# Convolution stage: the remainders of the weight tiles made by GpSimd in place of VectorE

## What is computed

```python
# second block, after the branch y_b (retention) is known up to its projection
u   = a * sigmoid(b)                       # a, b: two projections of the normalised x
c   = causal depthwise convolution of u, 31 taps per feature, + bias
c   = silu(layer_norm(c)) * silu(gate)     # gate: a third projection
y_a = c @ w_conv_proj
y_b = o @ w_ret_proj                       # o: 2048 features wide
m   = sigmoid(g_a) * y_a + sigmoid(g_b) * y_b
x   = x + m @ w_out
x   = rms_norm(x, final_gain)
```

## Time and profile before

| | us |
|---|---|
| median of 3 runs | 4187.54 |
| lowest, highest | 4186.81, 4188.52 |
| profiled execution | 4185.86 |
| its span, first to last instruction | 4184.1 |
| busy: PE | 4028.2 (96%) |
| busy: PEld | 3263.4 (78%) |
| busy: DVE | 2214.5 (53%) |
| busy: ACT | 1341.4 (32%) |
| busy: POOL | 1015.9 (24%) |
| mean granted clock of TensorE | 0.977 |

### The profile page before, as it was taken

One profiled execution on the slowest core, in us unless ns is written; L12 is line 12 of the kernel. 1 busy time (PEld: TensorE's weight loads), 2 busy tenths in 40 slices (PEclk: granted clock), 3 DMA queues, 4 the chain that ended last, 5 costly groups with the idle time before them and its releaser, 6 DMA issues. The chain is left out here.

```text
span 4184.1 us, 63976 instructions
## 1 busy us (share of the span) xinstructions
PE 4028.2 (96%) x26360; PEld 3263.4 (78%) x26360; DVE 2214.5 (53%) x2290; ACT 1341.4 (32%) x1621; POOL 1015.9 (24%) x533
## 2 busy tenths in 40 slices
PE   8999998999999999999999999999999999998799
PEld 6888777778888888877777878888888777776677
DVE  6644644552323232379986554343434477776873
ACT  4333443221212121233212123232323355546612
POOL 3222222333232323200002333132323122221221
PEclk9999999999999999999999999999999999998899
DMA  3111224121112121122333121111111222226641
GB/s 137 61 58 60 104 89 157 61 91 51 71 46 71 46 71 50 56 71 76 121 141 121 66 87 62 47 62 47 62 52 57 93 80 81 80 77 222 222 185 61
DMA packets 114613, 361.15 MB, mean 86 GB/s; under 512 B 12916, under 2 KB 14596, under 8 KB 114248
## 3 DMA queue, kind: packets, MB, share of 16 engines
q1 hardware_dynamic: 81216, 291.89, 20.2%
q10 hardware_dynamic: 33160, 65.72, 4.2%
HBM read 262.97 MB, written 94.58 MB: 85 GB/s over the span
## 5 line engine op out<-in xcount | busy, mean ns | idle before, releaser
L414 POOL CAST b_w_hi<-b_w 128x1024 fp32r<-128x1024 f32 x233 | 274.2, 1177 | 2768.4 <-PE ps L510 2123.5
L510 PE MATMUL ps<-b_hi,b_w_hi 128*128 128x512 f32 x1872 | 750.6, 401 | 25.8 <-DVE b_w_lo L430 11.4
L510 PE MATMUL ps<-b_lo,b_w_hi 128*128 128x512 f32 x1872 | 732.3, 391 | 0.0
L510 PE MATMUL ps<-b_hi,b_w_lo 128*128 128x512 f32 x1872 | 731.6, 391 | 0.0
L416 POOL TENSOR_TENSOR b_w_lo<-b_w,b_w_hi 128x1024 fp32r<-128x1024 f32 x233 | 600.6, 2578 | 18.7
L510 PE MATMUL ps<-h_hT_hi,b_w_hi 128*128 128x512 f32 x1216 | 490.8, 404 | 6.5 <-DVE h_hT_lo L240 4.6
L510 PE MATMUL ps<-h_hT_lo,b_w_hi 128*128 128x512 f32 x1216 | 475.5, 391 | 0.0
L510 PE MATMUL ps<-h_hT_hi,b_w_lo 128*128 128x512 f32 x1216 | 475.2, 391 | 0.0
L510 PEld LDWEIGHTS ps<-b_hi,b_w_hi 128*128 128x128 f32 x1872 | 353.2, 189 | 114.6 <-issue 35.0
L510 PEld LDWEIGHTS ps<-b_lo,b_w_hi 128*128 128x128 f32 x1872 | 353.6, 189 | 79.4 <-issue 8.4
L510 PEld LDWEIGHTS ps<-b_hi,b_w_lo 128*128 128x128 f32 x1872 | 353.4, 189 | 74.8
(11 more groups left out here) (703 smaller groups left out, 6332.6 us busy)
## 6 DMA issues: line engine op xcount, KB each, us to landing
b_w<-in_w SPq DMA_DIRECT2D x277, 512.0 KB, 3.5
scratch_x_park<-xT SPq DMA_DIRECT2D x24, 512.0 KB, 4.6
conv_room<-scratch_gate_park SPq DMA_DIRECT2D x24, 512.0 KB, 4.4
xT<-scratch_x_park SPq DMA_DIRECT2D x16, 512.0 KB, 11.7
scratch_gate_park<-ret_fill_out ACTq DMA_DIRECT2D x32, 256.0 KB, 2.0
scratch_o_park<-ret_o ACTq DMA_DIRECT2D x16, 512.0 KB, 4.0
scratch_gate_park<-rw_fill_out ACTq DMA_DIRECT2D x32, 256.0 KB, 2.1
scratch_sb_park<-rw_fill_out ACTq DMA_DIRECT2D x32, 256.0 KB, 2.0
```

The lines of the kernel that those rows point to most:

```text
L414: pool.tensor_copy(hi, w).then_inc(self.rounded, 1)
L510: ins = pe.matmul(out[:, t], w, y, start=start, stop=stop)
```

## The change

GpSimd's block no longer begins with a wait. It calls `subtract_tile` for the tiles first_tile+2 to o_tile_2+2, 33 of them, each as soon as ScalarE has rounded it, and goes on with `cut_tile` from o_tile_2+3. VectorE's block loses its three calls of `subtract_tile`, of which the first is in the loop and runs 31 times. The rounding stays with ScalarE. (L430 has 44 instructions in the whole execution; the other 11 are in other stages and aren't touched.)

```diff
--- before.py
+++ after.py
@@ -2221,7 +2221,8 @@
 
         @block.gpsimd
         def _(pool):
-            pool.wait_ge(stream.cut, o_tile_2 + 3)
+            for k in range(first_tile + 2, o_tile_2 + 3):
+                stream.subtract_tile(pool, k)
             for k in range(o_tile_2 + 3, out + KD):
                 stream.cut_tile(pool, k)
 
@@ -2399,7 +2400,6 @@
                 if e == 0:
                     for k in range(KD):
                         cut_o(k)
-                stream.subtract_tile(dve, first_tile + 1 + n)
                 if n % nt == 2 and n < tiles:
                     multiply(n // nt)
                 if e >= 1:
@@ -2411,9 +2411,7 @@
             for k in range(KD):
                 cut_o_2(k)
             add(KD - 1)
-            stream.subtract_tile(dve, o_tile_2 + 1)
             take_taps(taps, KD * taps_per)
-            stream.subtract_tile(dve, o_tile_2 + 2)
             for e in range(2):
                 add(KD + e)
             dve.wait_ge(mean_done, 1)
```

## The result

The changed kernel takes 4245.19 us in the median of four runs (4237.72 to 4253.02), against 4187.18 for the kernel before (4186.26 to 4188.52): ratio 1.0139 [1.012, 1.0157], 58 us slower. The forecast was 28 us slower, with a range that ended at 4229: the sign was right, half of the size was missing. The profiled execution, the lowest of the four, took 4237.72 us (span 4235.6), 51.9 above that of before.

What follows compares the result with a forecast made beforehand. VectorE was taken to bound the convolution stage, TensorE following. 64.2 - 33.9 - 1.0 + 2.9 - 4.2 = +28.0 us on 4185.86 gives 4213.9, with the median's 1.7 4215.6, said as 4215; range 4203 to 4229.

Steps and rivals of the forecast that it cites:

- VectorE's queue bounds the stage: Convolution stage, 1809 to 2174 us: VectorE's instructions and waits set its end, TensorE follows; any microsecond gained or lost moves the rest.
- Removed, 33.9 us: VectorE's chain from first tap to convolution end: 30 of the 33 remainders leave it, 1.13 us each.
- A stop costs some 2.14 us: VectorE's taps, two SBUF inputs: each GpSimd subtraction beside them was to cost VectorE's queue 2.14 us; ends 1.91 and 2.41.
- 64.2 - 1.0 + 2.9: Stall terms in the chain: 30 x 2.14, less one beside a PSUM addition, plus o_tile_2+3's cast and subtraction.
- a GpSimd subtraction takes 3.25 us even when it is held up: GpSimd's remainders: TensorE needs a tile only some 11.0 us after its slot is free, so was not to wait.
- VectorE busy without a gap: Sign in the profile: VectorE busy from 1809 us to the last L2105, whose end moves from 2174 to about 2202.
- TensorE's waits: Sign before the mean's matmuls: 11.4 us for L430 gone, all waits from 22.3 to about 50 us, behind ScalarE and before the mean.
- The wait at the cut of the branch output, -4.2 us: VectorE's wait at the first cut, for TensorE and ScalarE, was to vanish as these would be ahead: -4.2 us.
- rival 1: Convolution stage: taps aren't stopped, VectorE sheds 33.9 us, TensorE becomes the bound and regains 18.8 us: 4169; 3 in 100.
- Rival 3: Convolution stage: slower still, each remainder costs the whole 2.41 us, +8, or TensorE's slow spells show, +6: 4221 to 4229; 15 in 100.
- Rival 4: GpSimd's queue: it waits in order for each rounding, its later casts come late, at no extra cost; under 1 in 100.
- The end of the sum: Whole program: +28.0 us on the profiled 4185.86 gives 4213.9; the median of the runs is 1.7 higher, 4215.6.

## Why the prediction was half right

- **VectorE's queue bounds the stage**: right. 56 gaps of 0.11 us in the kernel before made the chain 6.3 us longer.
- **Removed, 33.9 us**: right. With the subtraction replaced by a write the chain lost 26.9, and 33.9 less the 6.6 us of a longer wait is 27.3.
- **A stop costs some 2.14 us**: right, with taps stopped in full at 3.36 to 3.47 us in the changed kernel. In the two kernels with few gaps, 32 instructions were stopped for 64.1 and 63.5 us, for the 66.1 that the sum had (64.2 - 1.0 + 2.9). The Trainium skill (SBUF — State Buffer, Who interferes with whom) says too that a GpSimd instruction which only writes doesn't contend; the 33 writes, with no tap over 1.300 us, bear that out.
- **Where it failed**: "a GpSimd subtraction takes 3.25 us even when it is held up, so TensorE doesn't wait for it". That row stands in a run of eight instructions of a tap's form that had begun only 3.45 us before (3967.74, the subtraction 3971.19). It was taken for the bound on how long GpSimd is held up, and is only a case of a short one. In the convolution, the 29 taps and the product between two final sums have no gap, and there the subtraction took up to 26.7 us, more than two tiles of TensorE.
- **"VectorE busy without a gap"** fell with it. The prediction took TensorE's lateness for something that VectorE's lateness makes; it also goes the other way. ScalarE evacuates only what TensorE has finished, and the unit's first taps hang on that. VectorE's waits inside the chain went from 5.6 to 37.3 us, and of the +50.3 they are 31.7.
- **TensorE's waits** were to grow from 22.3 to about 50 us, behind ScalarE and before the mean; they are 68.5, of which 46.5 for L430, the very line that was to be free.
- **Fewer stops than predicted**: 27, where the kernels with gaps have 32. As GpSimd waits, subtractions move into VectorE's idle times. The stops alone are 18.6 us net, where the sum had 32.2 (66.1 less 33.9), and this hides a part of the loss.
- **The wait at the cut of the branch output, -4.2 us**: it did not go, 4.3 us are left of it. It is gone in the three changed kernels with gaps, which fits that this term fell with the same step.
- **Rivals**: rival 1 was rightly thought unlikely, as taps are stopped. Rival 3 named the right side but with other causes (a whole 2.41 us each; slow spells of TensorE) and too small a price. Rival 4 asked whether GpSimd would be late, looked only at its last casts, and gave it nothing.
- **The end of the sum**: the profiled execution is 51.9 us above that of before, the median 58.0. The changed kernel's four runs spread over 15 us, where the four of before spread over 2; in the later measurements of the kernel before, 10 and 16 runs spread over 11 and 16. That the starvation depends on how the two queues happen to stand to each other would explain this, but one trace shows only one run of it.

**When a subtraction is passed, and what ends it.** In the traces of the six kernels in which GpSimd subtracts in this stage, 146 remainders come due while VectorE is busy. Count the VectorE instructions that have followed each other since the last gap, stop or addition from PSUM, the running one included: in 118 cases seven or fewer, and none of these subtractions was passed by another VectorE instruction with two SBUF inputs (longest 3.52 us); in 28 cases eight or more (up to 14), and 24 of these were passed, by 1 to 20 instructions. The traces also show what ended these 24 spells. In ten it was a gap, six of them the one before a final sum (L2105) and four made in the experiments. In nine it was the instruction right behind the product (L2366), as at 1837.95, though that one starts 1.13 us after the product without a gap. In five VectorE had run out of work. No subtraction was passed over any of the three.

**What is still open.** Why the line lies near eight, and why the place behind a product lets GpSimd in; the product is the only instruction of another form among the taps, but no run put another one there. The count doesn't decide it alone either. The subtractions due at 2067.70 in the changed kernel and at 2073.93 in that of the early tiles both come 0.25 us into the seventh tap after a stopped one. The first was served at the next boundary, in 3.29 us; the second was passed by 11 instructions. The 8 to 14 are counted from traces of this kernel's rhythm alone, and instructions of other lengths weren't tried.

## What to carry to other kernels

Before work that reads SBUF is moved from VectorE to GpSimd, ask two prices: what it stops on VectorE (here 2.14 us a subtraction against the 1.13 that it cost there), and how long it is kept out itself where VectorE runs two-input instructions without a gap; the second is not in the median but in the longest duration of its line, and it lands on whoever waits for the result. If such work has to be there, gaps help: one of 0.11 us before every eighth tap, or a single one in the middle of a unit's 29, held the longest subtraction to 6.1 or 10.5 us and gave back 25 to 26 us of the 58. Writes alone (zeros into 128x1024) stopped nothing here. And where one queue bounds a stage, look first at what holds up its first instruction and at its waits inside the stage: the two together were worth 10 us here, with the first tap 4.5 us earlier.

## What was not expected of the hardware

A GpSimd instruction that is due is not served at the next boundary between two VectorE instructions: with taps 1.20 us apart it was passed by up to 20 of them, 26.7 us for a subtraction that takes 2.4 alone. The Trainium skill (SBUF — State Buffer, Who interferes with whom) lets issue order decide who blocks; this case's traces agree for a subtraction that comes early in a run, and for 24 of the 28 that came at the eighth instruction or later they don't, as the first to come was served after others that came behind it. In the two executions with the early tiles on GpSimd and no gaps the pattern repeats through the first 21 subtractions: the first that is passed takes 23.45 us in both, with 17 instructions passing it. The 22nd subtractions are the pair told above, and there the two part. A pause of a tenth of a microsecond was enough to end a spell. And the cost of a stop didn't depend on how long GpSimd had waited: 3.36 us after 21 us of waiting, and here, in the changed kernel, after one:
```profile
2067.70 3.29 POOL L430 TENSOR_TENSOR b_w_lo<-b_w,b_w_hi 128x1024 fp32r<-128x1024 f32 x1 [8.43 <-ACT b_w_hi L424]
```
```profile
2068.65 3.41 DVE L2102 SCALAR_TENSOR_TENSOR conv_room<-conv_room,cols_sb 128x1024 f32<-128x1024 f32 x1
```
